# Differential attention as one stage: query-key panels inside the loop, row-wise outputs, per-row norm

## The reference

```python
qkv = einsum('bsd,de->bse', x, w_qkv)              # 1024 -> 3 x 1024
q, k: 8 heads x 2 components x 64;  v: 8 heads x 128
q = partial_rotary(q) * 64 ** -0.5;  k = partial_rotary(k)
s = q . k per component, key chunk of 64 <= query chunk of 64
a = softmax(s[0]) - lam * softmax(s[1])
o = rms_norm(a @ v, g_sub) * (1 - lam_init)        # per token and head
out = o.reshape(512, 1024) @ w_o
```

## Time and profile before

| | |
|---|---|
| median of 3 runs | 2739.46 us (2734.72 to 2742.97) |
| profiled execution | 2739.39 us, span on the core 2737.7 us |
| busy | PE 93%, DVE 38%, ACT 31%, POOL 34% |
| clock granted to PE, mean | 0.952 |
| attention, first projection matmul to first join matmul | 1425.73 to 1723.47 us |

### The profile page before, as it was taken

The page is one execution under the profiler, slowest core; times in us unless marked ns, Lnnn a source line. Parts: engine busy times, 40 slices in busy tenths (PEclk is TensorE's granted clock), DMA queues, the critical chain, the costliest instruction groups (busy, mean ns, idle before and its releaser), DMA issues.

```text
span 2737.7 us, 30359 instructions
## 1 busy us (share of the span) xinstructions
PE 2552.3 (93%) x12088; PEld 2026.1 (74%) x12088; DVE 1050.8 (38%) x1804; ACT 835.7 (31%) x1206; POOL 925.2 (34%) x706
## 2 busy tenths in 40 slices
PE   5999999889978988999999997999999899899997
PEld 4866777568658885887688743688888788788885
DVE  4533334235445544552328354431110442511103
ACT  3334433233423322334331343222231222222220
POOL 3422432143310000342145400244454355354452
PEclk9999999899989997999999967899999999999999
DMA  4322221032210000432232300123332133223231
GB/s 126 77 53 62 86 86 53 31 86 81 77 46 1 1 1 9 93 81 52 53 102 78 107 1 0 62 77 94 106 108 93 62 108 108 77 92 95 89 123 62
DMA packets 126390, 191.61 MB, mean 70 GB/s; under 512 B 24753, under 2 KB 70193, under 8 KB 126273
## 3 DMA queue, kind: packets, MB, share of 16 engines
q1 hardware_dynamic: 104960, 182.47, 22.2%
q10 hardware_dynamic: 21312, 7.46, 1.2%
HBM read 187.81 MB, written 2.10 MB: 69 GB/s over the span
## 4 chain that ended last, share of the span: by engine, by line
issue 66%; POOL 29%; PE 4%; DVE 1%; DMA 0%; POOLq 0%; ACT 0%; SPq 0%; ACTq 0%
POOL weights_low L563 29%; PE bank L587 1%; PE bank L588 1%; PE bank L589 1%; DMA weights_raw<-in_fox_w_in_dram 0%; POOLq L568 0%; DVE row_statistics L1843 0%; DVE x L1867 0%; DVE x L1869 0%; DVE x L1893 0%; POOLq L561 0%; ACT weights_high L1305 0%; SPq L470 0%; ACT L1305 0%; DVE row_statistics L1861 0%
## 5 line engine op out<-in xcount | busy, mean ns | idle before, releaser
L563 POOL TENSOR_TENSOR weights_low<-weights_raw,weights_high 128x512 fp32r<-128x512 f32 x688 | 922.5, 1372 | 1778.3 <-ACT weights_high L1305 1778.3
L587 PE MATMUL bank<-xt_high,weights_high 128*128 128x512 f32 (+1 forms) x1632 | 616.4, 378 | 17.8 <-POOL weights_low L563 9.4
L589 PE MATMUL bank<-xt_high,weights_low 128*128 128x512 f32 (+1 forms) x1632 | 607.4, 372 | 0.0
L588 PE MATMUL bank<-xt_low,weights_high 128*128 128x512 f32 (+1 forms) x1632 | 607.4, 372 | 0.0
L1305 ACT ACTIVATE weights_high<-weights_raw 128x2048 fp32r<-128x2048 f32 x172 | 329.2, 1915 | 799.2 <-PE bank L589 788.8
L587 PEld LDWEIGHTS bank<-xt_high,weights_high 128*128 128x128 f32 x1632 | 314.4, 193 | 85.9 <-POOL weights_low L563 15.9
L589 PEld LDWEIGHTS bank<-xt_high,weights_low 128*128 128x128 f32 x1632 | 313.4, 192 | 52.4
L588 PEld LDWEIGHTS bank<-xt_low,weights_high 128*128 128x128 f32 x1632 | 314.2, 193 | 49.2
L587 PE MATMUL bank<-weights_high,xt_high 128*128 128x512 f32 x512 | 205.7, 402 | 4.5 <-DVE xt_low L1880 2.1
L589 PE MATMUL bank<-weights_high,xt_low 128*128 128x512 f32 x512 | 200.7, 392 | 0.0
L588 PE MATMUL bank<-weights_low,xt_high 128*128 128x512 f32 x512 | 200.2, 391 | 0.0
(11 more groups left out here) (371 smaller groups left out, 3200.3 us busy)
## 6 DMA issues: line engine op xcount, KB each, us to landing
weights_raw<-in_fox_w_in_dram SPq DMA_DIRECT2D x64, 512.0 KB, 6.1
weights_raw<-in_ffn_w_gate_dram SPq DMA_DIRECT2D x44, 512.0 KB, 4.0
weights_raw<-in_ffn_w_up_dram SPq DMA_DIRECT2D x44, 512.0 KB, 4.9
weights_raw<-in_ffn_w_down_dram SPq DMA_DIRECT2D x40, 512.0 KB, 4.3
weights_raw<-in_gla_w_in_dram SPq DMA_DIRECT2D x24, 512.0 KB, 4.1
weights_raw<-in_gdn_w_in_dram SPq DMA_DIRECT2D x24, 512.0 KB, 4.4
weights_raw<-in_attn_w_qkv_dram SPq DMA_DIRECT2D x24, 512.0 KB, 4.4
weights_raw<-in_conv_w_in_dram SPq DMA_DIRECT2D x24, 512.0 KB, 4.6
```

The costliest lines, as they stand in the source:

```text
L563: pool.tensor_tensor(w_lo[:, odd, k], raw[:, odd, k], w_hi[:, odd, k].bitcast(F32), ALU.subtract)\
L587: pe.matmul(out_ap, lh, rh, start=first, stop=False)
L588: pe.matmul(out_ap, lh, rl, start=False, stop=False)
L589: return pe.matmul(out_ap, ll, rh, start=False, stop=last)
```

## The change

The three projections and the loop become one stage of six panels. The order is now: both value panels (rows, copied by ACT), a panel with queries and keys of heads 0 and 1, then the loop. The panels of heads 2 to 7 run inside it: `head_block_of(n)` names, for each even n below 24, one 128-column block, whose 24 matmuls PE runs ahead of `turn_pair(n)`. ACT copies a block (`take_head`), DVE rotates it (`rotate`) after `mix` of the next step. After the fourth block of a panel ACT makes both high parts of the next panel.

The scores use two bank pairs instead of three, and `pair_scores(n + 2)` now stands behind `turn_pair(n)`. `weigh_values` runs at every step and gives output rows: i + 1 matmuls of 128 columns with the transposed probabilities as weights. The norm sums squares along a row on DVE (`sum_heads`), takes the root as exp(-0.5 ln u) on ACT (`roots`, once for six heads at step 30, once at the end), and scales the rows (`normalise`). PE transposes the scaled rows (`rows_turned`), ACT and DVE write the high and low parts straight from the bank. The join waits for other events (`done`). The scratch buffers of the loop move to where the gated tiles go later. Indentation is cut by eight columns below.

```diff
+HEAD_ORDER = (0, 2, 1, 3)
+PAIRED = ((0, 0), (1, 0), (0, 1), (1, 1), (2, 0), (3, 0), (2, 1), (3, 1))
+def head_block_of(n):
+    if 0 <= n < 24 and n % 2 == 0:
+        return 3 + n // 8, n // 2 % 4
+    return None
...
-            project("attn_w_qkv_2", 0, 0, 2, False, "dve", "rotary A")
-            project("attn_w_qkv_2", 0, D, 2, False, "dve", "rotary B")
-            project("attn_w_qkv_2", 0, 2 * D, 2, True, "act", "copy C")
-            stage("attn", gated=KT, squares=8, norms=1, roots=1)
+            stage("attn", layer=0, pairs=6, full=18, gated=KT)
...
+                    elif n == 0 and st["attn"]:
+                        done = ((diff["exps"], 64), (diff["exps"], 64), (diff["out_taken"], 8), (gated_low, st["gated"]))[b]
+                        pe.wait_ge(*done)
...
-            all_free(st)
+            def head_block(p, pos, odd):
+                if not odd:
+                    c = 4 * (p - 2) + pos
+                    if c < 4:
+                        pe.wait_ge(diff["v_taken"], c + 1)
+                    elif c < 6:
+                        pe.wait_ge(diff["v_taken"], 8)
+                    else:
+                        pe.wait_ge(diff["copied"], c - 1)
+                dst = bank[pos] if p == 2 else bank[(4, 7)[pos % 2]]
+                piece(st["pair"] + p, HEAD_ORDER[pos], odd, dst, False)
             def pair_scores(n):
                 h, i = divmod(n, TT)
-                if n >= 3:
-                    pe.wait_ge(diff["exps"], 2 * n - 4)
+                pe.wait_ge(diff["rotated"], 2 * h + 2)
+                if n >= 2:
+                    pe.wait_ge(diff["exps"], 2 * n - 2)
                 keys = (i + 1) * P
                 for c in range(2):
-                    dst, rows = bank[2 * (n % 3) + c], slice(CHUNK * c, CHUNK * c + CHUNK)
+                    dst, rows = bank[2 * (n % 2) + c], slice(CHUNK * c, CHUNK * c + CHUNK)
                     pe.matmul(dst[:, 0:keys], buf_a[rows, h, i * P:i * P + P], buf_b[rows, h, 0:keys],
                               start=True, stop=False)
                     pe.matmul(dst[:, i * P:keys], ident_b[:], mask2_b[:], start=False, stop=True)\
...
                                        pair_probs[:, n % 2, 0, k * P:k * P + P], ident[:])
                 ins.then_inc(diff["turned"], 1)
-            def weigh_values(h):
-                pe.wait_ge(diff["turned_used"], TT * (h + 1))
-                if h:
+            def weigh_values(n):
+                h, i = divmod(n, TT)
+                pe.wait_ge(diff["turned_used"], n + 1)
+                if h and i == 0:
                     pe.wait_ge(diff["out_taken"], h)
-                for k in range(TT):
-                    ins = pe.matmul(bank[7][:, k * P:], c_rows[:, k, h * P:h * P + P],
-                                    probs_t[:, h % 2, k, k * P:], start=k == 0, stop=k == TT - 1)
-                ins.then_inc(diff["out_full"], 1)
+                for k in range(i + 1):
+                    ins = pe.matmul(bank[5][:, i * P:i * P + P], pair_probs_t[:, n % 2, k * P:k * P + P],
+                                    c_rows[:, k, h * P:h * P + P], start=k == 0, stop=k == i)
+                ins.then_inc(diff["weighed"], 1)
+            first_rows(st)
+            pe.wait_ge(dve_freed, st["dve"])
+            for b, odd in PAIRED:
+                piece(st["pair"] + 1, b, odd, bank[4 + b], True)
+            for pos, odd in PAIRED:
+                head_block(2, pos, odd)
             n_all = ATTN_HEADS * TT
-            pair_scores(0)
-            pair_scores(1)
+            pe.wait_ge(diff["copied"], 4)
+            for n in range(2):
+                pair_scores(n)
             for n in range(n_all):
+                if head_block_of(n):
+                    for odd in range(2):
+                        head_block(*head_block_of(n), odd)
+                turn_pair(n)
                 if n + 2 < n_all:
                     pair_scores(n + 2)
-                turn_pair(n)
-                if n % TT == 1 and n > TT:
-                    weigh_values(n // TT - 1)
-            weigh_values(ATTN_HEADS - 1)
-            norm_sums(st, list(range(8)), 8, bank[2])
-            pe.wait_ge(diff["selector"], 1)
-            pe.wait_ge(rows_r, st["norms"] + 1)
+                if n:
+                    weigh_values(n - 1)
+            weigh_values(n_all - 1)
             for h in range(ATTN_HEADS):
-                spread(st, h, diff["spread"], lambda n: n - 3, 8, bank[4 + h % 4])
+                pe.wait_ge(diff["normed"], h + 1)
+                if h >= 2:
+                    pe.wait_ge(gated_low, st["gated"] + h - 1)
+                for k in range(TT):
+                    ins = pe.transpose(bank[6 + h % 2][:, k * P:k * P + P], buf_d[:, h, k * P:k * P + P], ident[:])
+                ins.then_inc(diff["rows_turned"], 1)
...
+            def take_value(p, b):
+                wait_bank(act, st, p, b)
+                act.activation(c_rows[:, b, COLS * p:COLS * p + COLS], bank[4 * p + b][:], ACT.Copy)\
+                    .then_inc(diff["v_taken"], 1)
+            def take_head(p, pos):
+                c = 4 * (p - 2) + pos
+                wait_bank(act, st, p, pos)
+                if c:
+                    act.wait_ge(diff["rotated"], c)
+                src = bank[pos] if p == 2 else bank[(4, 7)[pos % 2]]
+                act.activation(rotary_in[:], src[:], ACT.Copy).then_inc(diff["copied"], 1)
...
+                act.activation(pair_probs_t[:, n % 2, 0:keys], bank[6][:, 0:keys], ACT.Copy)\
                     .then_inc(diff["turned_used"], 1)
...
+                act.wait_ge(diff["weighed"], TT * h + TT)
+                act.activation(buf_d[:, h], bank[5][:], ACT.Copy).then_inc(diff["out_taken"], 1)
+                act.wait_ge(diff["out_taken"], h + 1)
+                if h >= 2:
+                    act.wait_ge(diff["sums"], h - 1)
+                act.activation(pair_squares[:, h % 2], buf_d[:, h], ACT.Square).then_inc(diff["squares"], 1)
+            def roots(batch):
+                u, y = [pair_norms[:, m, (0, 24)[batch]:(24, 32)[batch]] for m in (0, 1)]
+                act.wait_ge(diff["logs"], batch + 1)
+                link(act.activation(y, u, ACT.Ln))
+                act.activation(y, y, ACT.Exp, scale=-0.5).then_inc(diff["roots"], 1)
+            for p in range(2):
+                take_value(p, 0)
+                take_value(p, 1)
+                weights_high(st["pair"] + p + 1, 0)
+                take_value(p, 2)
+                take_value(p, 3)
+                weights_high(st["pair"] + p + 1, 1)
+            take_head(2, 0)
+            take_head(2, 1)
+            weights_high(st["pair"] + 3, 0)
+            take_head(2, 2)
+            weights_high(st["pair"] + 3, 1)
+            take_head(2, 3)
             n_all = ATTN_HEADS * TT
             for n in range(n_all):
                 pair_exponentials(n)
                 if n:
                     take_pair(n - 1)
+                if head_block_of(n - 1):
+                    p, pos = head_block_of(n - 1)
+                    take_head(p, pos)
+                    if pos == 3:
+                        for odd in range(2):
+                            weights_high(st["pair"] + p + 1, odd)
                 if n % TT == 2 and n > TT:
                     take_out(n // TT - 1)
+                if n == 30:
+                    roots(0)
             take_pair(n_all - 1)
             take_out(ATTN_HEADS - 1)
-            act.wait_ge(diff["out_taken"], ATTN_HEADS)
-            square_tiles(st, [buf_d[:, h] for h in range(ATTN_HEADS)])
-            root(st, 0, scratch(st)["newton"][0:8])
+            roots(1)
             for h in range(ATTN_HEADS):
-                high(st, h)
+                act.wait_ge(diff["rows_turned"], h + 1)
+                act.activation(g_hi[:, h], bank[6 + h % 2][:], ACT.Identity, scale=cols[:, 1:2])\
+                    .then_inc(gated_high, 1)
...
+            def rotate(p, pos):
+                c, h = 4 * (p - 2) + pos, 2 * (p - 2) + pos // 2
+                dst, scale = (buf_b[:, h], 1.0) if pos % 2 else (buf_a[:, h], 64 ** -.5)
+                dve.wait_ge(diff["copied"], c + 1)
+                link(dve.stream_shuffle(rotary_sin[:], rotary_in[:], SWAP))
+                link(dve.scalar_tensor_tensor(dst, rotary_in[:], scale, rotary[:, 0], ALU.mult, ALU.mult))
+                link(dve.scalar_tensor_tensor(rotary_sin[:], rotary_sin[:], scale, rotary[:, 1],
+                                              ALU.mult, ALU.mult))
+                dve.tensor_tensor(dst, dst, rotary_sin[:], ALU.add).then_inc(diff["rotated"], 1)
+                dve.wait_ge(diff["rotated"], c + 1)
+            def sum_heads(h):
+                dve.wait_ge(diff["squares"], h + 1)
+                dve.reduce_sum(pair_norms[:, 0, TT * h:TT * h + TT], by_tile(pair_squares[:, h % 2]), AX)\
+                    .then_inc(diff["sums"], 1)
+            def mean_squares(batch):
```

(46 more changed lines are left out.)

54 lines of the change are left out of this document (24 added, 30 removed).

## The result

The changed kernel takes 2751.03 us (median of five runs, 2750.19 to 2752.19) against 2739.46 before. Side by side the ratio is 1.0043, interval 1.0028 to 1.0058: slower by 12 us where I had forecast 3 to 4 us faster, most likely no measurable change. The time lies inside the range, but the sign is not the one I gave most chance.

What follows compares the result with a forecast made beforehand. PE bounds the attention loop, at a clock that switches between 2.4 and 1.2 GHz. The loop with what precedes it loses 18 us, the tail gains 21.8, the join starts 3.6 earlier: 2739.4-3.6 = 2736 us, range 2710 to 2760.

Steps and rivals of the forecast that it cites:

- Opening and panels: Before the loop: opening panel gains 1.5 us, two more panels take 21.96 us each, first score at 1495.8.
- First block: Before the loop: score pairs 2.5 us, block 5.45, cold clock 2.3; first transposes at 1506.1.
- Odd steps: Loop steps without a block: PE idles before the transposes, 1.05 us in one odd step, 1.65 in the other.
- POOL-paced steps 8 and 16: Loop steps where blocks wait for POOL's low weight pieces: stall 3.3 us, twice (bounds 0 and 9).
- Clock: Loop gaps between blocks lose the clock: one fall a head, 5 x 3.2 = 16 us (bounds 0 and 36).
- Step 24: Loop step with no block following: 5.45 us less, 1.0 idle more; 0.4 at step 23 for waiting exponentials.
- Last eight steps: Last two heads, no blocks, clock 0.50: 42 us from transposes 24 to last weigh's end (bounds 31 and 44).
- Tail: Last weigh to join start: 8.1 us, where heads 0 and 1 suffice, against 29.9 before; gain 21.8.
- my two signs of being wrong: A tail over 12 us, or odd loop steps with no idle, would show the prediction wrong.
- weights late: Rival, chance 0.14: in the loop PE waits for weights from the block's start, stall 9 us, not 3.3; 2747 us.
- clock falls in both gaps: Rival, chance 0.21: PE starts each block in the loop at 0.50, 36 us instead of 16; 2756 us.
- Clock high: Rival, chance 0.22: blocks hold the loop's clock at 1.00; 2718 us, or 2707 if the last heads hold too.

Runs made afterwards that it cites:

- after: The changed kernel itself, set against the kernel before the change: 2751.03 us, ratio 1.0043.
- e2: Changed kernel with each head's tail transposes in its own bank, six heads normalised earlier, join waiting pair by pair: 2747.09 us, ratio 1.0026.
- e9: Changed kernel with the rotation of the last block moved behind the mix of pair 25: 2748.03 us, ratio 1.0043.
- e1: Changed kernel with scores of pair n+2 again ahead of the transposes of pair n: 2732.06 us, ratio 0.9976.
- e11: e1 with ACT copying a finished head's output out one step earlier: 2715.40 us, ratio 0.9907.
- e5: Changed kernel with all panels ahead of the loop, no blocks inside it, and scores again ahead of transposes: 2749.65 us, ratio 1.0081.
- e12: Changed kernel with the edits of e1, e2, e3, e9 and e11, and the first norm batch one step later: 2696.40 us, ratio 0.9834.
- e3: Changed kernel with the 24 matmuls of a block split over two steps, 12 in each: 2713.97 us, ratio 0.9906.
- e14: e3 with the tail of e2 and the late rotation of e9, transposes still ahead of scores: 2708.71 us, ratio 0.9880.

## Why the prediction went wrong

Two terms failed: the tail, sized at 8.1 us and 14.0 long, and the last rotation at step 24, put at nothing beside 0.4 us for the exponentials, where the step took 4.5 us more than the sum had. The reason for the clock's falls failed too, though its size came out. By the steps of the prediction, against the profile of after:

- *Opening and panels:* first score predicted 1495.8, measured 1496.7. The wait is for the fourth copy, behind the rotation of the third tile, as said.
- *First block:* first transposes predicted 1506.1, measured 1508.55. The clock is 0.50 from 1495 to 1505, and what I had sized at 2.3 us by the join's few matmuls cost about 4.
- *Odd steps:* predicted idle 1.05 and 1.65, measured 0.88 and 1.46. A head of undisturbed steps is 24.44 us (4.10 + 8.45 + 3.60 + 8.29, the last one from e2) against 24.2. Right.
- *POOL-paced steps 8 and 16:* stall predicted 3.3, measured 12.00 - 8.29 = 3.7. Right in length; of the idle of 3 us that I had named as its sign only 0.27 and 0.32 us show, since a fall of the clock fills the rest.
- *Clock:* predicted 16 us from 5 falls, measured 15.3 (steps 2, 4, 12, 14, 20 and 22 are 4.4, 3.0, 1.6, 1.6, 3.1 and 1.6 us longer than undisturbed ones) from eight falls, two of them hidden at POOL's steps. So six falls of 2.6 us on average stand for five of 3.2. That the size held is luck; the reason did not hold, see below.
- *Step 24:* predicted 0.4 for the exponentials, measured 4.5 more than the 4.2 of the sum. I had weighed the rotation only under a block ("fit under 5.45 us of block"); the last rotation has none to cover it, and falls together with POOL's split, beside which its operations take up to 1.64 us. e9 moves 2.6 of it, and the two slow operations of the mix are another 1.9.
- *Last eight steps:* predicted 42, measured 41.9.
- *Tail:* predicted 8.1, measured 14.0. The failed words are "where heads 0 and 1 suffice". They would, for the join's operands; but PE's program has the transposes of all eight heads ahead of the join, two banks for them, and so a low part between each two. e2 gives the join the banks that my sentence took for granted, with DVE's normalising moved ahead as well, and measures 7.9. A tail over 12 us was one of my two signs of being wrong.

Sum: 2.4 late at the start, 6.1 in steps 0 to 23, 5.9 in the tail, 14.4 at the join, and 2 us behind it. The sign turned on mis-sized terms of 4.5 and 5.9 us, in a balance of a 21.8 us gain and an 18 us loss that I had right to 9 us on one side and 6 on the other.

**The clock, where the reason failed.** I took the falls for a matter of the gap between blocks, dense or not, because of the fall at 100% busy, and set aside the Trainium skill's account of PE's idle gaps as one by which the loop would stay at 1.00. e1 and e11 speak against me: with the same gaps and the same work, five falls went when the wait of 1.05 us went. Rows 3 had been read in too narrow a window: 3 us ahead of that fall the timeline of the kernel before has

```profile
1598.65 0.66 PE L988 MATMUL bank<-identity,pair_probs 128*128 128x128 f32 x4 [0.66 <-DVE pair_probs L2137]
```

and there is a wait of that size at 1613.14, 1629.28 and 1643.77, each 1 to 3 us before a fall (1614 to 1615, 1631, 1645). The one at 1659.91 brought none. The same page of the Trainium skill, "TensorE: Matmul & The Clock Gate", has in its section on psum-queue depth-cycling that short idle moments of PE between groups of matmuls, if frequent enough, make the clock go back and forth. The runs agree, with falls behind waits of 0.66 us and more, though not behind every one. What neither that sentence nor idle alone explains is that in e5 the clock does not return for 27 us with PE 100% busy. What PE runs seems to count beside its waits: here the clock fell at waits, and it rose inside blocks or at the end of weighs, up to 1 us behind it.

Of the rivals "weights late" (2747) and "clock falls in both gaps" (2756) came nearest to the time, both by luck: the first by a stall of 9 us where 3.7 was measured, the second by too large a loss from the clock (36 against 15.3), and both with the tail and step 24 left as forecast. "Clock high" would have been right for the blocks as such: e12 shows them at 1.00, once almost nothing waits. The change's own idea, blocks inside the loop, is worth about what one could hope; what undid it was the score pair moved behind the transposes (e1 and e11: 36 us with the falls) or, the same loss covered in another way, 24 matmuls at every second step instead of 12 at each (e3: 37 us). The two overlap: e14 to e12 shows 6 us left for the order in a split loop, before step 24.

What stays open: why some waits of 0.66 to 1.54 us bring a fall and others don't, and the 2 us behind the join's start.

## What to carry to other kernels

Price a wait of TensorE in a loop of short matmuls at its length plus the clock it takes away, here 1 us plus 1.6 to 4.4, and look for waits in the few us ahead of a fall before blaming the work. When dense work is there to be spread, put some of it in front of every wait rather than much in front of every second. And before writing "where the first two suffice", read down the waiting engine's program order: what stands ahead of the instruction counts, whether it is needed or not.

## What the runs showed of the hardware

DVE is slower beside POOL's split: a 128x128 mix operation of 0.29 us takes 1.25 beside it, another of 0.35 also 1.25, and a 128x512 rotation operation of 0.69 takes 1.64. "Advanced Engine Details and Errata" of the Trainium skill (section on GPSIMD details) has the two share a read and a write interface. The trace agrees: in the loop of after the rotations that start at 1556, 1612 and 1669 are slow, and these are the three stretches of POOL's split. e9 moves the third out of it, and it runs at 0.69 again, while POOL's eight pieces take 9.90 us instead of 11.26. So both engines lose, DVE's small operations most, by a factor of about four. That they share an interface is the Trainium skill's account; the runs show the overlap and its cost. A matmul of 512 columns on plain 32-bit operands went as two instructions and took 0.89 us (7.09 for eight), that of the projections' type 0.27 (1.63 for six).
